# A hybrid conv/S5 block on one core: a new order of the opening, less VectorE work in block 0, ScalarE roundings at the end of the last block, and a moved tail

## What is computed

```python
mod = silu(c) @ w_ada + b_ada                 # six vectors: sh1, sc1, g1, sh2, sc2, g2
h = rmsnorm(x, norm1_g) * (1 + sc1) + sh1
u_conv, u_ssm, gl_conv, gl_ssm = split(h @ w_in)
y_conv = conformer_conv(u_conv)               # gate, 31 taps, layernorm, silu, projection
y_ssm = s5_mixer(u_ssm)                       # 32 groups of 64 complex states, gelu, GLU
x = x + g1 * ((sigmoid(gl_conv) * y_conv + sigmoid(gl_ssm) * y_ssm) @ w_out)
h = rmsnorm(x, norm2_g) * (1 + sc2) + sh2
f_gate, f_up = split(h @ w_ffn_in)
x = x + g2 * ((silu(f_gate) * f_up) @ w_ffn_out)
out = rmsnorm(x, final_g)
```

## Time and profile before

| | before |
|---|---|
| median of 3 executions | 2546.4 us |
| profiled execution | 2545.64 us, span 2543.8 us |
| PE busy | 2490.7 us, 98% of the span |
| DVE, POOL, ACT busy | 1643.7, 1738.1, 871.4 us |
| granted PE clock, mean | 0.992 |
| chain that ended last | PE 79%, DVE 12%, DMA 3%, issue 3%, ACT 2%, POOL 1% |

### The profile page before, as it was taken

How to read it: one execution, slowest core, us unless ns; L and a number is a source line. 1 busy time by engine, 2 the same in 40 slices (tenths; PEclk the granted TensorE clock), 3 DMA queues, 4 the chain that set the end, 5 groups by cost and what they waited for, 6 DMA issues and landing times.

```text
span 2543.8 us, 31372 instructions
## 1 busy us (share of the span) xinstructions
PE 2490.7 (98%) x11419; PEld 2050.3 (81%) x11419; DVE 1643.7 (65%) x2039; ACT 871.4 (34%) x1376; POOL 1738.1 (68%) x1192
## 2 busy tenths in 40 slices
PE   7999999999999999999999999999999999999997
PEld 3888788888888888888788888878888888888886
DVE  5989739945596648946833334485555336889795
ACT  4322411143012421146433345443223334445444
POOL 2776777677866777676887767787777764445555
PEclk9999999999999999999999999999999999999998
DMA  8666347553666347562332232324565337475533
GB/s 279 206 190 216 108 157 224 156 170 115 212 174 190 124 160 222 141 222 86 120 96 75 88 118 77 108 91 141 182 199 175 116 97 245 131 234 178 190 98 108
DMA packets 426161, 395.66 MB, mean 156 GB/s; under 512 B 92232, under 2 KB 330520, under 8 KB 424472
## 3 DMA queue, kind: packets, MB, share of 16 engines
q1 hardware_dynamic: 324688, 319.93, 40.2%
q10 hardware_dynamic: 101320, 73.72, 9.4%
HBM read 317.88 MB, written 67.24 MB: 151 GB/s over the span
## 4 chain that ended last, share of the span: by engine, by line
PE 79%; DVE 12%; DMA 3%; issue 3%; ACT 2%; POOL 1%; ACTq 0%; SPq 0%; DVEq 0%; POOLq 0%
PE bank L1909 18%; PE bank L1911 18%; PE bank L1910 18%; PE bank L2154 4%; PE bank L2156 4%; PE bank L2155 4%; DVE bank L836 3%; PE bank L2070 2%; PE bank L2068 2%; PE bank L2069 2%; DMA row_pair<-in_w_ffn_out 2%; DVE bank L1024 1%; DVE hid_lo L1053 1%; PE bank L1989 1%; PE bank L1974 1%
## 5 line engine op out<-in xcount | busy, mean ns | idle before, releaser
L2238 POOL TENSOR_TENSOR w_lo<-raw,w_hi 128x1024 fp32r<-128x1024 f32 x192 | 480.7, 2504 | 15.4
L2236 POOL CAST w_hi<-raw 128x1024 fp32r<-128x1024 f32 x192 | 209.0, 1089 | 362.4 <-PE bank L1911 277.0
L1909 PE MATMUL bank<-h_hi,w_hi 128*128 128x512 f32 x896 | 352.0, 393 | 0.9 <-ACT wm L1314 0.9
L1911 PE MATMUL bank<-h_hi,w_lo 128*128 128x512 f32 x896 | 349.6, 390 | 0.0
L1910 PE MATMUL bank<-h_lo,w_hi 128*128 128x512 f32 x896 | 349.3, 390 | 0.0
L836 DVE SCALAR_TENSOR_TENSOR bank<-uc,cwt,bank 128x512 f32<-128x512 f32 x464 | 323.1, 748 | 6.2
L2261 POOL TENSOR_TENSOR fw_lo<-fsum,fw_hi 128x512 fp32r<-128x512 f32 x176 | 235.7, 1342 | 74.8 <-ACT fw_hi L1596 74.8
L1909 PE MATMUL bank<-xc_hi_T,fw_hi 128*128 128x512 f32 x704 | 276.0, 392 | 5.6 <-DVE tr L1029 4.2
L1911 PE MATMUL bank<-xc_hi_T,fw_lo 128*128 128x512 f32 x704 | 274.3, 390 | 0.0
L1910 PE MATMUL bank<-xc_lo_T,fw_hi 128*128 128x512 f32 x704 | 274.2, 389 | 0.0
L2293 POOL TENSOR_TENSOR ow_lo<-raw,ow_hi 128x512 fp32r<-128x512 f32 x116 | 160.8, 1387 | 164.2 <-ACT ow_hi L1637 164.0
(11 more groups left out here) (340 smaller groups left out, 5245.8 us busy)
## 6 DMA issues: line engine op xcount, KB each, us to landing
raw<-in_w_in SPq DMA_DIRECT2D x112, 512.0 KB, 3.9
raw<-in_w_ffn_in SPq DMA_DIRECT2D x66, 512.0 KB, 5.8
hid_scratch<-tr SPq DMA_DIRECT2D x88, 256.0 KB, 3.2
raw<-tsum_scratch SPq DMA_DIRECT2D x66, 256.0 KB, 3.2
g2b<-in_w_ada SPq DMA_DIRECT2D x64, 256.0 KB, 3.6
ssm_m<-vk_scratch SPq DMA_DIRECT2D x32, 512.0 KB, 5.1
raw<-in_ssm_glu SPq DMA_DIRECT2D x32, 512.0 KB, 3.6
raw<-in_w_out SPq DMA_DIRECT2D x32, 512.0 KB, 3.7
```

The lines of the kernel that those rows point to most:

```text
L1909: t.matmul(dst, wh, xh, start=first, stop=False)
L1911: return t.matmul(dst, wl, xh, start=False, stop=last)
L2236: g.tensor_copy(hi[:], src[:]).then_inc(hi_done, 1)
L2238: g.tensor_tensor(lo[:], src[:], hi[:].bitcast(F32), ALU.subtract).then_inc(split_done, 1)
```

## The change

1. c gets a load and a turn of its own (`nat_c`, vc); silu (cs) is taken from it before the seven pieces of `nat_v` are issued. ACT's queue is now: c, a first Silu (pre), poles, log_dt, cs, `nat_v`, `nat_b`. x moves from ACT's queue to SP's, between slabs 2 and 3.
2. PE's order becomes vc, v1, v0, ada1, ada3, bx, ada5, h0 to h2, sums, ada7, mt; h3 to h7 are turned inside us0, each behind the hl of three tiles before, and v2 too. Slab 6 moves from PE to DVE. The opening's h use three banks, us0 starts on the fourth.
3. DVE does the pole chain ahead of the slabs' end, and the B work between slab 4 and slab 6; ACT does the exponentials and sines ahead of the norm. Odd h tiles are written once by ACT; DVE writes the second form in the bank.
4. Block 0: where the power is zero, `wm` and `vm` are copied (one instruction for three); `mag_k` is filled by ACT; the taps behind `ysl` grow from 14 to 22.
5. Last block: the hi part of the last six chunks is made by ACT (`out_high`), not POOL.
6. Tail: the squares of the last product move behind the loop, and alternate with the last three `weight_high`; POOL's gain multiplications move behind `ow_lo` of steps 150, 151 and 153; half rows are done pair by pair with `end_rows`.

```diff
-        pe_pro = ["v1", "ada1", "v0", "ada3", "ada5", "ada6", "ada7", "sums", "mt"] + h_steps[0:4] + ["bx"] + h_steps[4:] + ["v2"]
+        pe_pro = ["vc", "v1", "v0", "ada1", "ada3", "bx", "ada5"] + h_steps[0:3] + ["sums", "ada7", "mt"] + h_steps[3:] + ["v2"]
-        act_pro = ["cs", "dt"] + norm_act + [f"nx{i}" for i in R(TT)] + ["ej", "m8", "sj", "cj"] + h_act
+        act_pro = ["pre", "cs", "dt", "ej", "m8", "sj", "cj"] + norm_act + [f"nx{i}" for i in R(TT)] + first_act
-        CONV = [[tiles_01[:10], tiles_01[10:24], tiles_01[24:] + tiles_23[:-14], tiles_23[-14:]]]
+        CONV = [[tiles_01[:10], tiles_01[10:24], tiles_01[24:] + tiles_23[:-22], tiles_23[-22:]]]
...
+            act.dma_start(nat_c[:], c[0].rearrange("(k p) -> k p", p=P)).then_inc(c_in, 16)
+            act.wait_ge(x2_out[1], 1)
+            s.activation(sd[:, 0:1], half_pi[:], ACT.Silu).then_inc(*scal.step("pro", "pre"))
...
+            act.wait_ge(*tensor.after("pro", "vc"))
+            act.wait_ge(*scal.after("pro", "pre"))
+            s.activation(cact, bank[2][:, 0:KD], ACT.Silu).then_inc(*scal.step("pro", "cs"))
...
             dve.wait_ge(*tensor.after("pro", "bx"))
             link(v.tensor_tensor(b1[:], first, by_h(qr), ALU.mult))
             link(v.tensor_tensor(ptmp[:], first, by_h(qi), ALU.mult))
+            norm_root("pro")
+            slab_sum(6)
...
+                if k % 2:
+                    dve.wait_ge(*scal.after("pro", f"hh{k}"))
+                    turned = bank[plan["pro", f"h{k}"]][:]
+                    link(v.tensor_scalar(turned, turned, scale[0][:, k:k + 1], mod[:, k:k + 1], ALU.mult, ALU.add))
+                    low(h_lo[:, k, :], turned, h_hi[:, k, :], "pro", f"hl{k}")
+                else:
+                    h_split("pro", k)
...
+            def out_high(w):
+                act.wait_ge(raw_in[w % RAW], 16 * ((NB - 1) * (NW // RAW) + w // RAW + 1))
+                act.wait_ge(*chunk_used[NB - 1][w - SPL])
+                s.activation(w_hi[w % SPL][:], raw[w % RAW][:], ACT.Copy).then_inc(out_hi_done, 1)
...
+            for i, n in enumerate(R(N2 - HR + OW, N2)):
+                final_stat(NG - 1, 0, i)
+                weight_high(n)
+            final_stat(NG - 1, 0, TT - 1)
             final_root(NG - 1, 0)
-            for i, n in enumerate(R(N2 - HR + OW, N2)):
-                weight_high(n)
-                half_row(i)
-            half_row(TT - 1)
-            for n in R(len(ENDS)):
+            for n, (lo_, hi_) in enumerate(ENDS):
+                for i in R(lo_, hi_):
+                    half_row(i)
                 end_rows(n)
...
                         if b == 0 and name == "us0":
                             pe.wait_ge(*vec.after("pro", f"hl{k}"))
+                            if k + 3 < KD:
+                                transposes("pro", k + 3)
...
+                for i in {N2 - 4: [0], N2 - 3: [1], N2 - 1: [2, 3]}.get(n, []):
+                    pool.wait_ge(final_act, 5 * (2 * NG - 2) + i + 1)
+                    g.tensor_tensor(x3[0][i][:], x3[0][i][:], fgb[:], ALU.mult).then_inc(half_scaled_g, 1)
...
+                if n == 3:
+                    for i in R(TT):
+                        sp.dma_start(xs[:, i, :], x_d[i * P:(i + 1) * P, :]).then_inc(xs_in, 16)
```

More of the change, by code:

```diff
@@ L327, in build @@
         h_act = [n for k in R(KD) for n in (f"hh{k}", f"h{k}")]
+        first_act = [n for k in R(KD) for n in ((f"hh{k}",) if k % 2 else (f"hh{k}", f"h{k}"))]
         h_dve = [f"hl{k}" for k in R(KD)]
@@ L443, in build @@
                     plan[st, n] = z % 4
+                    if st == "pro":
+                        plan[st, n] = z % 3
+                    elif st == 0 and n[:2] == "us":
+                        plan[st, n] = (z + 3) % 4
                     z += 1
@@ L674, in _ @@
             slab_sum(0)
[L675 to L678, removed]
+            dve.wait_ge(*tensor.after("pro", "v1"))
+            for cols in (slice(0, 6 * KD), slice(7 * KD, nv_rows)):
+                link(v.tensor_copy(vt[:, cols], bank[1][:, cols]), "vt")
             dve.wait_ge(*tensor.after("pro", "v0"))
@@ L689, in _ @@
             angles(jarg[:, 0, :, :], jarg[:, 1, :, :], jtmp[:], th, T + 1, "jargs")
[L690 to L698, removed]
+            link(v.tensor_tensor(t0, ar, ar, ALU.mult))
+            link(v.tensor_tensor(t1, ai, ai, ALU.mult))
+            link(v.tensor_tensor(den, t0, t1, ALU.add))
+            link(v.reciprocal(den, den))
+            slab_sum(2)
             dve.wait_ge(*scal.after("pro", "cj"))
@@ L790, in _ @@
             reduce_turns()
-            dve.wait_ge(*scal.after("pro", "m8"))
-            link(v.tensor_copy(mag_k[:, :, 1:], mag_t[:].unsqueeze(2).broadcast_to([P, G, NC])))
             gated(0, 2)
@@ L1279, in h_tile @@
                 turned = bank[plan[stage, f"h{k}"]][:]
-                for dst, step in ((h_hi[:, k, :], f"hh{k}"), (turned, f"h{k}")):
+                for dst, step in ((h_hi[:, k, :], f"hh{k}"), (turned, f"h{k}"))[:1 if stage == "pro" and k % 2 else 2]:
                     s.activation(dst, turned, ACT.Identity, scale=scale[which][:, k:k + 1],
@@ L1306, in _ @@
             s.activation(jer[:], jarg[:, 1, :, :], ACT.Sin, bias=half_pi[:, 0:1]).then_inc(*scal.step("pro", "cj"))
+            norm_stats("pro", 64)
+            act.wait_ge(*vec.after("pro", "nr"))
+            for i in R(TT):
+                s.activation(xs[:, i, :], xs[:, i, :], ACT.Copy, scale=rs[:, i:i + 1]).then_inc(*scal.step("pro", f"nx{i}"))
             act.wait_ge(pro_v, mark["scale0"])
@@ L1319, in angle_turns @@
             def angle_turns():
+                act.wait_ge(*scal.after("pro", "m8"))
+                s.activation(mag_k[:, :, 1:], mag_t[:].unsqueeze(2).broadcast_to([P, G, NC]), ACT.Copy)\
+                    .then_inc(*scal.step(0, "mk"))
                 act.wait_ge(pro_v, mark["angles"])
```

147 lines of the change are left out of this document (75 added, 72 removed).

## The result

| | before | after |
|---|---|---|
| median of 20 executions each, in turn on one chip | 2545.36 us (2541.42 to 2550.97) | 2548.48 us (2546.67 to 2558.09) |
| span of the profiled execution | 2543.8 us | 2546.8 us |
| PE, DVE, ACT, POOL busy | 2490.7, 1643.7, 871.4, 1738.1 us | 2487.3, 1644.8, 876.0, 1728.0 us |

The ratio is 1.0016, 95% interval 1.0010 to 1.0022: the changed kernel is slower by 0.16%, 4 us (the medians differ by 3.1). I forecast 2540 with a range of 2532 to 2547. The result lies outside it, on the other side of the kernel before.

A forecast was written before the change was run, and what follows sets the result against it. PE's matmuls were taken as the bound, with gains only where PE stands still or runs at half rate. Opening +1.9, block 0 +0.8, last block -1.0, tail -8.2 gave -6.5 us: 2539.1, or 2540 against the median; range 2532 to 2547.

The forecast's parts named there:

- Tail: End of the kernel: PE runs through without its wait for ow_lo, -8.2 us, bounds -9.5 and -4.
- hid_lo of 153 comes at 2516.76 + 0.68, just in time: Tail: DVE's last hid_lo is ready for PE's need at 2517.4, so PE runs through from 2516.0 to 2524.2.
- ACT's sum: Tail: ACT is the path, root at 2518.1, then half rows and squares, last right halves from 2529.8, 8.8 before 2538.64.
- Rival 4: Tail: DVE or POOL holds it, every lock delays the combines; the tail gives 4 us, 2544; chance 0.10.
- Opening: Start to us0's end: norming x moves onto the path, half rate in us0; +1.9 us, bounds -2 and +5.
- Slab 3 had x ahead of it before too in effect: Opening: x's new queue buys no landing time; slab 3 taken at 22.5, bounds 21 and 23.2.
- Rival 2: Opening: the clock falls twice, sums and ada7 start at half rate; 3 us more, 2543; chance 0.19.
- Rival 1: Opening gains: slab 3 at 21 or sooner, PE at full rate in us0; 4 us better, 2536; chance 0.20.
- Rival 3: Opening: vector rows land late, each microsecond of v1 past 14.5 costs one, up to 2556; chance 0.07.
- Block 0: First block: ys_lo wait goes, the stall moves to s13, half clock falls on za2; +0.8 us, bounds -1.1 and +1.8.
- End of the last block: PE's w_lo waits of 2.8 us go, but the feed-forward part then waits; -1.0 us, bounds +0.5 and -2.8.
- Rival 5: End of the last block: the DVE-POOL locks go and it gives all 2.8 us, 2538; chance 0.08.

The follow-up runs named there:

- run 3: Changed kernel with all four of POOL's gain multiplications behind the last ow_lo: 2548.87 us, ratio 1.0009.
- run 5: Changed kernel with POOL's four gain multiplications waiting until DVE's last hid_lo is done: 2545.27 us, ratio 1.0002.
- run 10: Changed kernel with gains behind last hid_lo, 14 taps behind ysl, norm_root ahead of bx, then DVE replacing POOL's gains and ACT's half rows: 2538.18 us, ratio 0.9970.
- run 6: Changed kernel with POOL's four gains as one-input multiplications by 1: 2545.75 us in one execution.
- run 14: Changed kernel with x loaded from ACT's queue behind the seven pieces of nat_v, not from SP's: 2545.45 us in one execution.
- run 13: Kernel of run 10 with x loaded behind slab 3 and not ahead of it: 2536.67 us, ratio 0.9964 against the kernel before.
- Run 11: Kernel of run 10 with the opening of the kernel before: 2534.80 us, ratio 0.9957 against the kernel before.

## Why the prediction was wrong, step by step

**Tail: -8.2 forecast, -0.4 measured** (29.2 to 30.1, mean 29.6, in six executions, against 30.4 and 29.7 in two with the old tail, so no gain clear of the spread). This is the step that failed. The roundings came as I said (2.72 apart), ow_lo of 153 was in time, and behind step 150 PE waited only 0.48 us. What failed is "hid_lo of 153 comes at 2516.76 + 0.68, just in time". That time was read off the old trace, in which POOL stood idle beside the last part of DVE's chain (the 2.79 us ahead of its ow_lo of 151, until ACT rounded); the change closed POOL's work up under it. Counted from the last rounding, DVE's last hid_lo then ended at 11.0 us instead of 4.1. Runs 3 and 5, one wait apart, show that it was the gains: behind hid_lo, they give 3.9 of the missing 7.8 us back. Another part was missed in ACT's sum, which took the gains of POOL as ready: the half rows waited 2.25 and 1.15 us for them even in run 5, and with both given to DVE (run 10) the tail is 9.3 us shorter than 30.4, more than I had forecast. Rival 4 had the mechanism, with 4 us left of the gain and a chance of 0.10; 0.4 was left.

The rule that I had weighed at the end of the last block, of the Trainium skill ("SBUF — State Buffer", Who interferes with whom), says that a VectorE instruction with two SBUF inputs and a GpSimd instruction that reads SBUF block each other for the whole instruction. The rows of run 3 agree: 2.48, 2.71, 2.82 against gains of 2.66. So do DVE's instructions with an operand in a bank, which take 0.70 beside POOL's ow_lo. Run 6 agrees only in part (1.52 us beside an instruction of 3.0 with one input). Not run was a tail with all of DVE's side moved out of SBUF.

**Opening: +1.9 forecast, +3.8 measured** (seven executions, mean 60.5; four of the old opening, 56.4 to 57.1, mean 56.75; within my bounds of -2 and +5). The chain of waits was right, the size of the term was not. "Slab 3 had x ahead of it before too in effect" was right: with the old opening slab 3 started at 22.6 to 23.2. But its first number, 22.5, was too low: with x in SP's queue ahead of it slab 3 started at 23.4 to 24.1 in ten executions, beyond my bound of 23.2. And it could have been much lower: with x issued later from ACT's queue it started at 20.73 (run 14), and with x behind it right behind slab 1, so that bx began at 25.04 and not at 28.61 as in run 10 (run 13). The Trainium skill ("DMA: Bandwidth & Descriptors", Issuing engines are not separate DMA queues) says that the transfers of all issuing engines share the 16 DMA engines. The runs don't speak against it. I took from it that x's place buys nothing; runs 13 and 14 show that it matters which bytes are issued ahead of slab 3. The half rate in us0 was there. Rival 2 (the clock falls before sums) did not happen: ada7 took 3.60 for eight matmuls, as at full rate. Rival 1 (slab 3 at 21 or sooner) needs x elsewhere, and even then us0 ended at 57.5 and 57.9, not earlier than with the old opening. Rival 3 (vector rows late) did not happen: v1 came at 14.2, within my 14.5, and behind it and ada1 PE still stood 2.66 us for slab 3.

**Block 0: +0.8 forecast, +0.35 measured, and right only by chance.** From us0's end to m_hi there are four groups of executions: 14 taps and the long alternation 244.8 to 245.3 (four), 14 and short 242.9 to 243.0 (four), 22 and short 245.2 to 245.3 (six), 22 and long 248.5 and 248.8 (two). Run 11 has all the other edits of block 0 and belongs to the first group (245.14), so it is the taps. They cost 2.3 us in the short and about 3.6 in the long alternation, where I had 0.8 for all of block 0; and the profiled execution after was in the short alternation, worth 2.1 us with 14 taps and 3.4 with 22, which I didn't see at all. Two unseen terms cancelled. The steps themselves (the wait for ys_lo goes, the one for the sum stays) came as said, and the wait for the sum was 2.36 and not 4.7 because of the alternation; in the long one it was 6.89.

**End of the last block: -1.0 forecast, -0.7 measured** (939.2 us from m_hi to the first feed-forward rounding, in thirteen executions with ScalarE's roundings, against 939.6 to 940.0 in three without). The 2.8 us of waits for w_lo went and the feed-forward part gave most of it back at its start. Rival 5 did not happen.

**The sum by measured means:** 3.8 + 0.3 - 0.7 - 0.4 = +3.0 us, against +3.1 by the medians and +4 by the ratio. The feed-forward part, which no experiment touched, took between 1270.1 and 1274.9 us in the fourteen executions with the moved tail, and the 0.8 us of the table above lies within that. Each kernel was profiled once, and this spread is as large as most of the terms. The lower end of my range wasn't what it was said to be either: rival 1 with the tail's best bound is 2536 less 1.3, 2534.7, and not 2532.

## What to carry to other kernels

When a change closes up one engine's work, ask which engine it now runs beside, and take nothing of that engine's durations from a trace in which the first stood idle: here 0.69 us became 2.8. A wait that is moved out of the way shows the next one, and the engine to ask for it is the one with two SBUF inputs while POOL works; either order them by a semaphore, or give both jobs to one engine in one instruction, which was worth more here than all of the change. Bytes that aren't needed yet belong behind the load on which the chain hangs, whatever queue they are in.

## What the runs showed of the hardware

- A DVE instruction on 128x4 took 2.33 us beside POOL's gains (0.16 elsewhere): its length is POOL's, not its own.
- Beside a POOL instruction with one input, of 3.0 or 3.2 us, DVE's hid_lo took 0.8 us longer than alone, both times, and not as long as POOL's (run 6, one execution).
- In the changed kernel's tail DVE's instructions with an operand in a PSUM bank took 0.69 to 0.70 us beside POOL's ow_lo, and those with both inputs in SBUF up to 2.88 beside the gains.
- DVE and POOL, each with a period of 5.4 us in the scan, were in one of two patterns in the sixteen profiled executions. In the ten of the short one POOL started 3.5 us behind DVE, in the six of the long one 1.9 to 2.1 us. The choice goes with up to 3.4 us of block 0. What sets the offset wasn't tried.
